# Reordering the first loads of a second stage against the last store of the first, and other addresses for eight weight buffers

## The reference

```python
def block(xb):                       # 128 tokens at a time
    qry = (xb @ w_q).reshape(TB, PEER_HEADS, PEER_D_KEY)
    s1 = jnp.einsum('thd,nd->thn', qry[..., :half], keys_1)
    s2 = jnp.einsum('thd,nd->thn', qry[..., half:], keys_2)
    v1, i1 = lax.top_k(s1, K); v2, i2 = lax.top_k(s2, K)
    cand = (v1[..., :, None] + v2[..., None, :]).reshape(TB, PEER_HEADS, K * K)
    sc, ci = lax.top_k(cand, K)
    idx = (take_along_axis(i1, ci // K) * PEER_N_KEYS + take_along_axis(i2, ci % K))
    gate = softmax(sc)
    act = gelu(einsum('thed,td->the', u_table[idx], xb))
    return einsum('the,thed->td', gate * act, v_table[idx])
```

## Time and profile before

| | us |
|---|---|
| median of three runs | 1458.32 |
| the three runs | 1455.82, 1458.32, 1459.24 |
| profiled execution, its own time | 1460.59 |
| its span in the trace | 1458.8 |

### The profile page before, as it was taken

The page is one execution under the profiler, slowest core; times in us unless marked ns, Lnnn a source line. Parts: engine busy times, 40 slices in busy tenths (PEclk is TensorE's granted clock), DMA queues, the critical chain, the costliest instruction groups (busy, mean ns, idle before and its releaser), DMA issues.

```text
span 1458.8 us, 24697 instructions
## 1 busy us (share of the span) xinstructions
PE 1427.0 (98%) x8813; PEld 1367.2 (94%) x8813; DVE 1186.6 (81%) x2337; ACT 636.7 (44%) x1035; POOL 765.1 (52%) x428
## 2 busy tenths in 40 slices
PE   7999889999999999999999999899999999999998
PEld 6879678888999999999999999799999999999998
DVE  5747563388989999989999997588898998998994
ACT  4463472222433333447777775332243343433332
POOL 2524171233677678865545554256566665566630
PEclk9999999999999999999999999999999999999999
DMA  7400211312579989999999999989999999999991
GB/s 270 152 30 1 115 35 43 112 62 73 165 259 343 327 299 364 404 377 341 372 357 358 355 403 390 376 292 411 410 412 409 410 410 410 410 411 410 410 357 58
DMA packets 165902, 423.15 MB, mean 290 GB/s; under 512 B 13348, under 2 KB 85924, under 8 KB 163912
## 3 DMA queue, kind: packets, MB, share of 16 engines
q1 hardware_dynamic: 119624, 254.48, 46.8%
q0 software_dynamic: 46208, 167.81, 30.2%
HBM read 376.00 MB, written 46.20 MB: 289 GB/s over the span
## 4 chain that ended last, share of the span: by engine, by line
PE 90%; DMA 5%; DVE 2%; issue 1%; ACT 1%; SPq 0%; DVEq 0%; ACTq 0%
PE banks L2048 32%; PE banks L1812 16%; PE banks L2119 10%; PE banks L2121 10%; PE banks L2120 10%; PE banks L2087 5%; DMA act_in<-act_scratch 3%; DMA u_raw<-in_uT 2%; PE banks L2027 1%; PE banks L1842 1%; PE banks L1886 1%; PE banks L1944 1%; DVE x_res L1631 1%; PE banks L1964 1%; PE banks L1963 1%
## 5 line engine op out<-in xcount | busy, mean ns | idle before, releaser
L818 POOL DMA_INDIRECT rows<-in_v,idx x160 | 283.3, 1771 | 192.9 <-DVE x_res L1631 130.7
L2119 PE MATMUL banks<-w_hi,v_hi 128*128 128x352 f32 x1024 | 330.0, 322 | 1.9 <-DVE w_lo L1730 1.9
L2120 PE MATMUL banks<-w_lo,v_hi 128*128 128x352 f32 x1024 | 329.3, 322 | 0.0
L2121 PE MATMUL banks<-w_hi,v_lo 128*128 128x352 f32 x1024 | 329.3, 322 | 0.0
L1157 ACT ACTIVATE v_hi<-v_raw 128x1024 fp32r<-128x1024 f32 x128 | 134.4, 1059 | 287.4 <-DMA v_raw<-in_v 277.8
L818 POOL DMA_INDIRECT rows<-in_u,idx x160 | 191.1, 1195 | 124.7 <-DVE z L1613 91.1
L794 POOL TENSOR_TENSOR u_lo<-u_raw,u_hi 128x1024 fp32r<-128x1024 f32 x66 | 163.9, 2487 | 95.1 <-ACT u_hi L1052 47.9
L2048 PE MATMUL banks<-h_hi,u_hi 128*128 128x352 f32 x1024 | 191.3, 329 | 6.9 <-ACT act_kept L1078 6.9
L2048 PE MATMUL banks<-h_lo,u_hi 128*128 128x352 f32 x1024 | 198.0, 328 | 0.0
L2119 PEld LDWEIGHTS banks<-w_hi,v_hi 128*128 128x128 f32 x1024 | 192.3, 188 | 2.8 <-issue 2.6
L2120 PEld LDWEIGHTS banks<-w_lo,v_hi 128*128 128x128 f32 x1024 | 192.3, 188 | 0.0
(11 more groups left out here) (284 smaller groups left out, 2084.0 us busy)
## 6 DMA issues: line engine op xcount, KB each, us to landing
u_raw<-in_uT SPq DMA_DIRECT2D x128, 512.0 KB
v_raw<-in_v SPq DMA_DIRECT2D x128, 512.0 KB
gate_scratch<-stage SPq DMA_DIRECT2D x11, 2048.0 KB
gate_pairs<-gate_scratch SPq DMA_DIRECT2D x15, 1408.0 KB, 18.4
act_scratch<-act_out SPq DMA_DIRECT2D x116, 176.0 KB
act_in<-act_scratch SPq DMA_DIRECT2D x29, 704.0 KB
wi_raw<-in_w_in SPq DMA_DIRECT2D x8, 1024.0 KB, 6.9
wq_raw<-in_w_q SPq DMA_DIRECT2D x8, 1024.0 KB, 5.5
```

Source lines behind the costliest of these rows:

```text
L818: nc.gpsimd.indirect_dma_start(ROW_KB[U_SLOT[s]][:], None, a["u"] if kind in "ab" else v_flat, bass.IndirectOffsetOnAxis(ap=at_x, axis=0)) ...
L2119: mm(y, v_hi[x][:, ds], w_hi[q][:, j, :], start=start, stop=False)
L2120: mm(y, v_hi[x][:, ds], w_lo[q][:, j, :], start=False, stop=False)
L2121: return mm(y, v_lo[x][:, ds], w_hi[q][:, j, :], start=False, stop=stop)
```

## The change

The last store of stage 0 (`save_gates(5, 0)`) is left out of the last trip of `main` and comes after `post_load_u(120)`, so behind the loads of u 122, 123 and 124. v 0 and 1 now lie at 62 and 66 and wait for `z_done` at 120 in place of `gate_saved[0]`. The wait for `gate_saved[0]` stands with the others before the load `gates`. v 2 and 3 (now at 38 and 42, in stage 0) come after `post_load_u(123)`. v 4 and 5 (46, 50) wait for nothing more; v 6 and 7 have the addresses and the waits that they had.

```diff
--- before.py
+++ after.py
@@ -349,7 +349,7 @@
         U_NTH = [U_SLOT[:s].count(U_SLOT[s]) for s in range(len(ORDER))]
         U_BEFORE = [max([x for x in range(s) if U_SLOT[x] == U_SLOT[s]], default=None) for s in range(len(ORDER))]
 
-        V_KB = (38, 42, 46, 50, 62, 66, 54, 58)
+        V_KB = (62, 66, 38, 42, 46, 50, 54, 58)
         v_raw = [at(f"v_raw{x}", kb, [P, D]) for x, kb in enumerate(V_KB)]
         v_lo = [at(f"v_lo{x}", kb, [P, D], F32R) for x, kb in enumerate(V_KB)]
         v_hi = [at(f"v_hi{x}", kb, [P, D], F32R) for x, kb in enumerate((70, 74, 78, 82, 134, 138, 142, 146))]
@@ -618,14 +618,14 @@
                 sp.dma_start(gate_d[:, :, bass.ds(i * 2 + chunk, 1)].rearrange("g p o n t -> p g (o n t)"),
                              stage[chunk][:].rearrange("p (g n) t -> p g (n t)", n=PAIR)).then_inc(gate_saved[chunk], 16)
 
-            def main(i):
+            def main(i, last=False):
                 for j in range(MAIN_BODY):
                     n = i * MAIN_BODY + (PRE + j)
                     wait_ulo(sp, i, PRE + j, MAIN_BODY)
                     load_u(n + 4, j)
                     if not isinstance(n, int) or n - 2 < SAVED:
                         save_act(n - 2, j + 2)
-                    if j == MAIN_BODY // 2 + 1:
+                    if j == MAIN_BODY // 2 + 1 and not last:
                         save_gates(i, 0)
                     if j == 1 and not (isinstance(i, int) and i == 0):
                         save_gates(i - 1, 1)
@@ -636,7 +636,7 @@
             main(0)
             with sp.Fori(1, MAIN_TRIPS - 1) as i:
                 main(i)
-            main(MAIN_TRIPS - 1)
+            main(MAIN_TRIPS - 1, last=True)
 
             def load_v(n, x):
                 sp.dma_start(v_raw[x][:], a["v"][bass.ds(n, 1)].rearrange("o p d -> (o p) d")
@@ -660,22 +660,26 @@
                 load_u(n + 4, n % 4)
 
             post_load_u(POST)
+            save_gates(MAIN_TRIPS - 1, 0)
             post_load_u(POST + 1)
-            sp.wait_ge(gate_saved[0], 16 * (CHUNKS + 1) // 2)
+
+            sp.wait_ge(z_done, POST)
             for b in range(2):
                 load_v(SAVED + b, b)
             post_load_u(POST + 2)
-            for b in range(2, 4):
-                load_v(SAVED + b, b)
             for q in range(RING):
                 sp.wait_ge(act_saved[q], 16 * SAVED // RING)
             sp.wait_ge(gate_saved[1], 16 * (CHUNKS // 2))
+            sp.wait_ge(gate_saved[0], 16 * (CHUNKS + 1) // 2)
             sp.dma_start(gates[:].rearrange("p c n t -> p c (n t)"), half_pair(SAVED // PAIR, 1)).then_inc(gates_in, 16)
             post_load_u(POST + 3)
+            for b in range(2, 4):
+                load_v(SAVED + b, b)
             load_pair(NK // PAIR - 1, 0)
             for b in range(4, V_RING):
-
-                sp.wait_ge(z_done, (POST, POST, E_BLOCKS - 1, E_BLOCKS)[b - 4])
+                if b >= V_RING - 2:
+
+                    sp.wait_ge(z_done, E_BLOCKS - V_RING + 1 + b)
                 load_v(SAVED + b, b)
 
             def second(p, r, pair):
```

## The result

The changed kernel took 1450.31 us, the median of 20 runs (1444.94 to 1461.10), against 1459.25 us of the kernel before, run beside it (20 runs, 1452.38 to 1465.94). The ratio is 0.9947, with a 95% interval of 0.9930 to 0.9963: faster by 0.5%, some 8 us. I had forecast 1455.3, in a range of 1452.3 to 1457.8. Direction right, size too small by more than half, median outside the range.

A forecast was written before the change was run, and what follows sets the result against it. PE was taken to bound the kernel (90% of the span). The last third of block 125 at 945.8, plus 1.33 and 7.6, gave 954.7 against 957.66: 3.0 us gained, 1458.32 - 3.0 = 1455.3 us, range 1452.3 to 1457.8.

The forecast's parts named there:

- by the pace of 4.0 us a block: PE, blocks before 120: counting back 4.0 us a block from 916.56 puts the end of block 118 at 912.4.
- late loads here are a matter of bytes ahead, not of late issues: DMA queue, 902 to 942 us: engines busy throughout (share 1.03, 397 GB/s), so bytes queued ahead make u 122 and 127 late.
- the first wait: PE's idle time before block 120, for u 122 behind the stage 0 store: 2.19 us, predicted to go.
- the first wait is mostly moved into the second: PE, blocks 120 and 125: the 2.19 us wait goes, but the later one only shrinks from 4.70 to 4.2 us.
- the upper bound: End of block 127: at most 9.3 us gained, if it ended 8 x 4.0 us after 916.56, at 948.4.
- The case of bytes shared evenly: Gates' load beside gathers: shared by bytes, its 0.72 MB would pass in 3.6 us and u 127 be in time.
- More than one stall goes: Change of stage: gates' load starts before the gathers' burst, u 127 lands by 936, no half clock; 4 to 9 us gained; chance 0.20.
- Bytes kept: Loads at the change of stage: same bytes land by 942.1, v 3 last; gain 0 to 2 us; chance 0.18.
- slower: SP ahead of the gates' load: the store lands late and holds SP; at 938, 1462.8 us; chance 0.07.
- 0.50 for faster: Whole kernel: chance of a measurably faster result, 0.30 from the forecast plus 0.20 from "More than one stall goes".

The follow-up runs named there:

- e5: The kernel before, unchanged, traced once more: 1458.53 us.
- e4: The kernel before with only the loads of v 2 and 3 moved behind u 127, the store left in its old place: ratio 0.9970.
- e8: The kernel before, unchanged, traced once more: 1458.55 us.
- e1: The kernel before, unchanged, traced a second time: 1462.04 us.
- e7: The changed kernel with the gates' load last, behind u 127 and v 2 and 3: ratio 0.9945 to the kernel before.
- e11: Against e10: gates' load right behind u 127, `u_lo` 127 ahead of the weights on DVE, weights' rounding ahead of v's on ACT: 1442.66 us, ratio 0.9888.
- e10: The changed kernel with u 126 and 127 ahead of all v and gates loads, rounding and splitting of v 0 to 3 moved later: ratio 0.9949.
- e9: The changed kernel, unchanged, traced a third time: ratio 0.9929 to the kernel before.
- e2: The changed kernel, unchanged, traced a second time: ratio 0.9944 to the kernel before.
- e3: The changed kernel without the move of v 2 and 3: ratio 0.9967 to the kernel before.

## Why the prediction was right or wrong

**Right, for the execution it was made against.** No wait before block 120; the store issued near 907 (907.63), landed by 921 to 924 (gates' load issued 923.55); u 127 at 939.5 (938.8); block 125 at 941.0 (940.41); the last third of block 125 near 945.8 (945.24), with the half clock, not `u_lo` 125, as what held it; the second product at 954.7 to 955.1 (954.28); the second product no longer than before (495.7 us before, 495.8 after, from its first matmul to the end of its last). A gain of 3.0 was forecast and 3.3 of span measured.

**The step that failed** is "by the pace of 4.0 us a block", and with it the sentence that the sum is made against one profiled execution and then carried to the median. The pace belongs to an execution. At the quick one PE wants u 122 at 907 and not at 917, and the wait before block 120 is 6.0 to 7.2 us where I had 2.19. The store's place then costs those, the half clock after them, and DMA engines that run short for want of an issue. I had written "late loads here are a matter of bytes ahead, not of late issues". That is true at the slow pace, where the share is 1.03. At the quick one with the store in its old place it is true of the first wait alone: after it the engines stand nearly idle for some 4 us (share 0.22 from 918 to 922 in e5), and the share from 912 to 938 is 0.90 (e5) or 0.82 (e4). So "the first wait is mostly moved into the second" is also wrong there: alone the store's move shortens the first product by 4.4 us at the quick pace (583.2 to 578.8).

The clue stood in my own rows. Block 124 took 4.0 us, blocks 126 and 127 took 7.6 us together, 3.8 each, for the same 24 matmuls at full clock. I used both numbers in one sum and didn't ask why they differ.

**Slips in the sums.** Eight blocks of 4.0 us after 916.56 end at 948.56, so the upper bound was a gain of 9.1 us and not 9.3, and 4.0 us before 916.56 is 912.56 and not 912.4 (ACT rounded u 122 at 912.63). Neither moves the forecast. The case of bytes shared evenly is called the second rival, but that rival, as written, is about the order of the gates' load and the gathers.

**The rivals.** "More than one stall goes", at 0.20, had the size (4 to 9 us) and named the missing half clock. Its mechanism, the gates' load ahead of the gathers' burst, is not what happened: the DMA engines were as full as ever (share 1.03), and PE was early. "Bytes kept" and "slower" didn't come true; SP left the gates' load at 923.55, far from 930.

**The chances.** 0.50 for faster was cautious, and the range was narrow since it took a spread of 3.4 us in three runs for noise about one value. Twenty runs of each spread over 14 us (before) and 16 us (changed).

**Left open.** What decides the pace. In all five slow traces it begins with the first gate matmuls among those of the first product (648 us, 644 in e8); before that all thirteen have 158 ns. It can change at a wait of PE, also at a short one (e1 went from slow to quick after 1.8 us of waiting and e7 from quick to slow after 0.66, the first trace of before stayed slow after 2.2, e5 came out of a wait slow). No experiment was made on its cause. Whether its odds differ between kernels can't be told from five traces of one and three of the other.

## What to carry to other kernels

Compare two traces of the same kernel before costing an edit by microseconds: count the instructions of the bounding engine in a stretch where it never idles, and if two counts differ, make the sum at each pace. Where loads are asked for when a consumer is done, a faster consumer turns a short wait into a long one; what an edit to the queue is worth must be reckoned for the earliest arrival, not for the one in the trace. Ahead of the last loads that a stage needs nothing should stand that the next stage needs, on the DMA queue and on every in-order engine between the load and its user: a part of that (the change) gave 0.5%, all of it (e11) 1.1%, here.

## What the runs showed of the hardware

Two paces of PE at full clock, 158 and 167 ns for a matmul of 352 columns with its weight load, kept for more than 250 us: the granted clock is 1.00 and PE busy throughout at both, and only the count of matmuls and the distance between their starts tell them apart.

The clock after a wait is likewise not one thing. A wait of 2.8 us near 198 us, in the attention, was followed by a stretch at half clock in the first trace of before and in most others, and by none in e4, e7 and e8, whose first product began at 367 us and not at 371. These three also lack a second stretch near 273 us that nine of the other ten have. Whether the two stretches are all of the 4 us is not shown: e10 lacks the second one and began at 371.28. The same window in the first trace and in e8:

```profile
198.00:206.00 8.00, 5.22 (x23) 4.31 (x22) 3.35 (x15) 6.29 (x14) 7.29 (x2) 0.79 0.00 0
```

```profile
198.00:206.00 8.00, 5.50 (x29) 4.15 (x30) 4.08 (x16) 6.26 (x16) 7.92 (x3) 1.00 0.00 0
```

In blocks 120 to 127 waits of 3.0 us (e9) and of four times 1.5 to 2.5 us (e2) left the clock at full, while one of 2.8 us (e7) and all of 3.3 us and more were followed by half clock. After the waits of 3.31 us (e3) and 3.80 us (e4) it fell only when PE had run its first eight matmuls again, 1.4 us into the work. So which waits bring it is not told by their length alone here.
